# Bias products of a spatial gating unit moved to the layer's beginning, in a two-layer trunk with gated mixer branches and a hierarchical MoE

## What is computed

```
h  = rmsnorm(x, norm1_g)
p  = h @ w_in                     # 2304 columns, for four branches
A  = gelu(u) * z                  # spatial gating unit, chunks of 128 tokens, 4 groups of 64 channels
     z[t, g, c] = sum_{s <= t} w_s[g, t, s] * v[s, g, c] + b_s[g, t]
B  = attention with a window of 128 (4 query heads, 2 key heads of 64, QK norm, rotary, sinks)
C  = gated convolution with 3 taps
D  = GLU, convolution with 31 taps, layernorm over 256 channels, silu
m  = sum_b sigmoid(h @ w_gate + b_gate)_b * (y_b @ w_branch[b])
x  = x + m @ w_o
x  = x + moe(rmsnorm(x, norm2_g)) # top 1 of 4 groups, then top 2 of 4 experts in it
```

## Time and profile before

| | |
|---|---|
| median of 3 runs | 784.68 us (784.68 to 784.87) |
| the profiled execution's own time | 784.63 us |
| its span, first to last instruction | 782.9 us |
| TensorE busy | 772.4 us, 99% |
| VectorE busy | 646.9 us, 83% |
| ScalarE busy | 508.1 us, 65% |
| mean granted TensorE clock | 0.999 |

### The profile page before, as it was taken

The page is one execution under the profiler, slowest core; times in us unless marked ns, Lnnn a source line. Parts: engine busy times, 40 slices in busy tenths (PEclk is TensorE's granted clock), DMA queues, the critical chain, the costliest instruction groups (busy, mean ns, idle before and its releaser), DMA issues.

```text
span 782.9 us, 13142 instructions
## 1 busy us (share of the span) xinstructions
PE 772.4 (99%) x4850; PEld 690.5 (88%) x4850; DVE 646.9 (83%) x847; ACT 508.1 (65%) x592; POOL 22.6 (3%) x36
## 2 busy tenths in 40 slices
PE   8999999999999999999999999999999999999997
PEld 7899999999878888888889999999988888888885
DVE  5868898469689999897874799757968998989895
ACT  7625646655588778786643655565569877878772
POOL 4020000000000000000001000000000000000000
PEclk9999999999999999999999999999999999999999
DMA  9867254266719999998365624526562999999971
GB/s 303 273 215 241 83 201 137 94 216 216 269 54 328 346 383 335 386 338 276 119 214 204 225 97 173 162 72 239 212 234 90 334 365 386 336 363 352 354 262 54
DMA packets 79499, 186.76 MB, mean 239 GB/s; under 512 B 12470, under 2 KB 24408, under 8 KB 79448
## 3 DMA queue, kind: packets, MB, share of 16 engines
q1 hardware_dynamic: 79448, 186.08, 67.0%
HBM read 185.01 MB, written 1.05 MB: 238 GB/s over the span
## 4 chain that ended last, share of the span: by engine, by line
PE 96%; DVE 1%; ACT 1%; DMA 1%; issue 1%; POOL 0%; DVEq 0%; SPq 0%; ACTq 0%; POOLq 0%
PE bank L1380 28%; PE bank L1382 28%; PE bank L1381 28%; PE bank L1774 2%; PE bank L1685 2%; PE bank L1800 1%; PE bank L1662 1%; PE bank L1539 1%; DMA x<-in_x 1%; PE bank L1445 1%; PE bank L1448 0%; PE bank L1560 0%; PE bank L1564 0%; PE bank L1655 0%; PE bank L1769 0%
## 5 line engine op out<-in xcount | busy, mean ns | idle before, releaser
L839 DVE TENSOR_TENSOR w_lo<-raw,w_hi 128x2048 fp32r<-128x2048 f32 (+1 forms) x144 | 313.5, 2197 | 56.4 <-ACT w_hi L522 55.8
L522 ACT ACTIVATE w_hi<-raw 128x2048 fp32r<-128x2048 f32 (+1 forms) x144 | 264.1, 1844 | 135.3 <-PE bank L1382 131.4
L1380 PE MATMUL bank<-a_hi,w_hi 128*128 128x256 f32 x688 | 195.8, 285 | 0.6 <-DVE a_lo L905 0.6
L1381 PE MATMUL bank<-a_hi,w_lo 128*128 128x256 f32 x688 | 194.6, 283 | 0.0
L1382 PE MATMUL bank<-a_lo,w_hi 128*128 128x256 f32 x688 | 194.6, 283 | 0.0
L1380 PE MATMUL bank<-w_hi,y_lo 128*128 128x512 f32 x432 | 170.9, 395 | 0.0
L1382 PE MATMUL bank<-w_lo,y_lo 128*128 128x512 f32 x432 | 168.6, 390 | 0.0
L1380 PEld LDWEIGHTS bank<-a_hi,w_hi 128*128 128x128 f32 x688 | 131.9, 192 | 1.6 <-issue 1.5
L1381 PEld LDWEIGHTS bank<-a_hi,w_lo 128*128 128x128 f32 x688 | 132.0, 192 | 0.1
L1382 PEld LDWEIGHTS bank<-a_lo,w_hi 128*128 128x128 f32 x688 | 132.0, 192 | 0.0
L1381 PE MATMUL bank<-w_hi,y_hi 128*128 128x512 f32 x288 | 112.3, 390 | 0.0
(11 more groups left out here) (309 smaller groups left out, 970.4 us busy)
## 6 DMA issues: line engine op xcount, KB each, us to landing
raw<-in_w_e_gate SPq DMA_DIRECT2D x63, 512.0 KB, 4.9
raw<-in_w_e_up SPq DMA_DIRECT2D x63, 512.0 KB, 6.5
raw<-in_w_gate SPq DMA_DIRECT2D x56, 512.0 KB, 4.5
mid<-in_w_e_down SPq DMA_DIRECT2D x54, 512.0 KB, 6.1
raw<-in_w_in SPq DMA_DIRECT2D x32, 512.0 KB, 6.6
raw<-in_w_e_down SPq DMA_DIRECT2D x18, 512.0 KB, 5.0
raw<-in_w_branch SPq DMA_DIRECT2D x16, 512.0 KB, 4.1
raw<-in_w_o SPq DMA_DIRECT2D x16, 512.0 KB, 4.4
```

The source lines that it names most:

```text
L522: a.activation(w_hi[:, at.part(n), 0:w], raw_at(slot)[:, 0:w], ACT.Copy).then_inc(hi_done, 1)
L839: v.tensor_tensor(w_lo[:, part, 0:w], raw_at(slot)[:, 0:w], w_hi[:, part, 0:w].bitcast(F32), ALU.subtract).then_inc(split_done, 1)
L1380: mm(ps, a2[0], b2[0], start=first, stop=False, skip_group_check=shared)
L1381: mm(ps, a2[1], b2[0], start=False, stop=False, skip_group_check=shared)
```

## The change

The four bias products of a layer leave the spatial gating unit. They are issued at the end of `parameter_columns`, behind the transposes of the small parameters, into bank 7. Only the first has `start=True`. The products of the gating unit then add to what is there. Ahead of them stands a wait for all low halves of h.

Bank 7 is now taken from there to the gating unit. So the transposed queries and keys of the second half of the tokens go to bank 4. Bank 4 holds the transposed spatial weights until VectorE has masked them, hence a wait for sgw_done ahead of these transposes.

```diff
+        QK_BANKS = (6, 4)
...
                 for t in range(T):
                     act.wait_ge(S("qk_tp"), T * l + t + 1)
-                    a.activation(qk_t[:, t, :], bank[6 + t][:, 0:384], ACT.Copy).then_inc(S("qk_t_done"), 1)
+                    a.activation(qk_t[:, t, :], bank[QK_BANKS[t]][:, 0:384], ACT.Copy).then_inc(S("qk_t_done"), 1)
...
                     last.then_inc(S("cols_tp"), 1)
+                    pe.wait_ge(S("h_lo_done"), KT * (l + 1))
+                    for c in range(CT):
+                        for t in range(T):
+                            o = SEQ * c + P * t
+                            mm(bank[7][:, o:o + P], sgsel[:, P * c:P * c + P], sgb[:, :], start=c == 0 and t == 0, stop=False,
+                               skip_group_check=True)
...
                 pe.wait_ge(S("qk_done"), l + 1)
+                pe.wait_ge(S("sgw_done"), l + 1)
                 for t in range(T):
                     for i in range(NH // 2):
-                        last = tp(bank[6 + t][:, P * i:P * i + P],
+                        last = tp(bank[QK_BANKS[t]][:, P * i:P * i + P],
...
                 for c in range(CT):
                     for t in range(T):
                         o = slice(SEQ * c + P * t, SEQ * c + P * t + P)
-                        mm(bank[7][:, o], sgsel[:, P * c:P * c + P], sgb[:, :], start=True, stop=False,
-                           skip_group_check=True)
                         for j in range(2):
```

## The result

The changed kernel is slower: 787.79 us, the median of 10 runs (786.37 to 789.60), against 784.88 for the kernel before beside it (784.57 to 787.08). The ratio is 1.0032, with a 95% interval of 1.0020 to 1.0044. The forecast was 786.6, in the range 785.6 to 787.9.

What follows compares the result with a forecast made beforehand. The prediction took TensorE, busy for 99% of the span, to bound the kernel. It added 2 x 1.08 us and saved 0.26, so +1.90 us on the median of 784.68 gave 786.6 us, range 785.6 to 787.9.

Steps and rivals of the forecast that it cites:

- The gating unit: TensorE's gating unit keeps only 64-column products in one stream: 1.02 us instead of 3.13, saving 2.11 us a layer.
- The layer's beginning: Eight 4-row records between the last transpose and the next unit add 1.08 us a layer, bounds 0.88 to 1.74.
- rival 2: Moved products at the layer's beginning are cheaper, 0.88 us a layer: 786.2 us, no change that can be told; chance 0.24.
- the drain: At the layer's beginning, going from 40 to 4 rows drains TensorE: 1.08 us with it, 0.88 without.
- The edits costed at nothing: Bank 4 for three transposes, and added waits for masked spatial weights and low halves of h, cost no time.
- The wait for the taps: TensorE's sum over channels waits for VectorE's copy, starting 0.14 us after it; about 1.9 us a layer lost, 0.26 saved overall.
- rival 1: The wait for VectorE's taps before the sum over channels doesn't bind: 2.06 us come off, 782.6 us; chance 0.09.
- The delay is not absorbed: The 1.08 us added at each layer's beginning also delays the scores and VectorE, so slack doesn't take it up.
- The sum: Over both layers, 2 x 1.08 us added and 0.26 saved: +1.90 us, giving 786.6 us.
- rival 3: Moved products at the layer's beginning never fill up, each spacing 0.22 us: +3.22 us, 787.9 us; chance 0.03.
- rival 4: TensorE's new wait lowers its clock to 1.2 GHz for one gate unit, 5.8 us a layer: 798 us; chance 0.02.

Runs made afterwards that it cites:

- The 40 rows: The changed kernel with both operands of the bias products zero-padded to 40 rows: ratio 1.0017, 786.4 us in runs at granted clock 0.999 or more.
- one reordering: The changed kernel with VectorE making unit 22's low part after the copy signalling the taps' end: ratio 0.9984, 782.6 us in runs at clock 0.999 or more.
- the kernel with the extra products: The kernel before with four more bias products a layer at the layer's beginning, the gating unit keeping its own: 789.26 us, ratio 1.0054.
- the one stream: The kernel before with the four bias products in one stream at the head of the gating unit: ratio 0.9997, 784.3 us in runs at clock 0.999 or more.

## Why the prediction was right, point by point

- **The gating unit.** 1.02 us forecast, 1.02 measured, 2.11 saved. (The prediction calls the 64-column ones sixteen products; they are sixteen records of eight products. The sum counts records and holds.)
- **The layer's beginning.** 1.08 forecast, 1.09 measured, between the bounds of 0.88 and 1.74. Eight records of 4 rows run like any others, and the dear part is the first spacing and the way out. The 40 rows show that the step in is one of the edges, 0.1 us, so rival 2's low bound of 0.88 was out of reach as the products stand; even with 40 rows 0.97 us is added (1.13 less 0.16). The prediction had the low bound follow once the drain is gone, and that is only half of it: the long first spacing stays. The Trainium skill (TensorEngine Tiling (Array Packing), Key Properties) says that a change of the tiling mode drains TensorE. For the step in, the traces agree: 0.16 from 40 to 4 rows and 0.07 from 40 to 40.
- **The edits costed at nothing** were nothing: 784.71 against 784.7 for the banks and the wait for the masked weights. The wait on the low halves of h shows nowhere either: 0.16 us lie between the last transpose and the stream, the step that the prediction gave.
- **The wait for the taps.** Forecast: the sum starts 0.14 us behind the copy; 0.15 measured. 1.9 us lost a layer; 1.86 by the starts, or 1.7 in the view of waits, which counts from the end of the last record. VectorE's stretch of 39.6 us unchanged. Both the sign and most of the size hang on this step, and the cause was right. Undoing it by one reordering gave rival 1's 782.6 us to the tenth.
- **The delay is not absorbed:** forecast 2.16 us for two layers, 2.14 in the trace of the kernel with the extra products.
- **The sum.** +1.90 forecast, +1.8 at full clock. The ratio of all runs, 1.0032, is 2.5 us, and the medians are 2.9 apart. At full clock this is the mechanism and its size. For the median of all runs, part of the hit is luck: 787.79 lies 0.1 us below the upper end of the range, 787.9, and that end came from rival 3, which had nothing to do with it; the changed kernel run again took 787.99.
- **The clock.** The term that was mis-sized is rival 4's. I had it as a fall behind the new wait, with a chance of 0.02. In truth falls were there in half of the kernel before's runs already, at other places. The one profile that I had was of an execution without one, and so was each of the three runs shown. They came more often after the change, and that added about 0.7 us to the ratio. Its rows say less than the prediction took from them. In the earlier trace rows the view gives 1.00 from 5 to 10 us, but TensorE's first records, of 128 columns, start 0.21 us apart up to 7 us, and like ones 0.11 apart after it, so TensorE ran at the lower level at first. From the timeline of the kernel before:

```profile
3.71 2.55 PE L1393 MATMUL bank<-ones 128*128 128x128 f32 x11
...
11.00 0.83 PE L1393 MATMUL bank<-ones 128*128 128x128 f32 x6
```

And that trace does hold a fall, at its end. TensorE's last record ends at 778.9:

```profile
779.00:781.80 2.80, 0.00 (x0) 1.00 0.95 360
781.80:782.90 1.10, 0.00 (x0) 0.53 0.10 37
```

The Trainium skill (TensorE: Matmul & The Clock Gate, Part 1), which I cited for an idle TensorE, names 1.2 GHz as its level, and this end agrees. The falls that cost time don't follow an idle TensorE: they stand behind stretches in which it was over 90% busy, in short records.

What stays open: what sets the share of runs with a fall. The kernel with only the extra products had a clock below 0.999 in all of its 6 runs and no new wait at all, so the wait isn't needed for it. Both kernels shift the second layer against the first, but nothing here tested that alone.

## What to carry to other kernels

On an engine that is busy all the time, a saved stretch is worth only the margin of the next wait behind it. Look for the waits that the profile does not name, because they were in time by 0.4 us, and at how busy the other engine is from its last own wait to the signal; if it is full, the gain stops there, and an addition elsewhere counts in full. Then look in that queue for one instruction that nobody needs soon: here one moved split turned 1.8 us lost into 2.1 us gained. And group TensorE's products by their shape before moving them: the one stream was worth 1 us a layer, and the place nothing.

## What the runs showed of the hardware that was not expected

- A change of the rows that a product uses costs TensorE three times. The step in takes 0.16 us from 40 to 4 rows, and 0.07 from 40 to 40. The first spacing is 0.21 us with 4 rows and 0.19 with 40, instead of 0.11. The way out to a full-width product is 0.20. Padding 4 rows to 40 took only the first of these away (1.13 instead of 1.25 us for eight records).
- TensorE's granted clock fell to 0.51 of its full level for about 3.5 us in single executions while TensorE was busy, behind stretches of short records (from 218.00 to 221.70: 3.39 of 3.70 us busy). Each time costs about 1.4 us, more than half of the difference that was to be measured here.
- Through two waits of 1.7 us (129.40 to 131.10, 500.50 to 502.20) it stayed at 1.00. Behind the last record, with TensorE idle for 2.9 us, it fell (0.53 from 781.80 to 782.90). At the program's start the view says 1.00 where the spacing of records, 0.21 instead of 0.11 us, says the lower level.
